# A hybrid diffusion backbone on one core: gate panels of the HGRN2 heads moved two heads back, the heads' read-out turned a head later

## The reference, cut to what matters

```python
q, zf, zb, v, g = split(h @ w_in)             # five parts of 1024 columns, 128 of each per head
log_f = log(lb + (1 - lb) * sigmoid(z)); k = (1 - lb) * sigmoid(-z)     # for zf and for zb
q = silu(q)
o = scan(q, kf, v, log_ff) + flip(scan(flip(q), flip(kb), flip(v), flip(log_fb)))
o = rmsnorm(o, gn_w)                          # over the 128 columns of each head
y = (o * silu(g)) @ w_out
```

## Time and profile before

| what | value |
|---|---|
| median of three runs | 2356.78 us (2351.39 to 2359.17) |
| the profiled execution, its own time | 2360.58 us |
| its span, first to last instruction | 2358.3 us |
| around the span | 2.3 us |
| mean granted TensorE clock | 0.948 |
| TensorE busy | 2155.7 us, 91% |
| VectorE, ScalarE busy | 1092.3 and 844.7 us |
| head panels and scans | from 75 to 609 us |
| output product | from 609.6 us on |

### The profile page before, as it was taken

How to read it: one execution, slowest core, us unless ns; L and a number is a source line. 1 busy time by engine, 2 the same in 40 slices (tenths; PEclk the granted TensorE clock), 3 DMA queues, 4 the chain that set the end, 5 groups by cost and what they waited for, 6 DMA issues and landing times.

```text
span 2358.3 us, 34131 instructions
## 1 busy us (share of the span) xinstructions
PE 2155.7 (91%) x13412; PEld 1918.5 (81%) x13412; DVE 1092.3 (46%) x1596; ACT 844.7 (36%) x1281; POOL 46.6 (2%) x72
## 2 busy tenths in 40 slices
PE   5999998997899999999999599999997598999998
PEld 3888888886789999999999597777774487888887
DVE  5654455556453222222234657667666435333334
ACT  2543334443224331122222344637373324542222
POOL 1000000000000000000000100000000000000000
PEclk8999999998899999999999799999998599999999
DMA  7322221221323332234321121211111232332332
GB/s 283 104 76 78 73 81 55 81 72 54 116 81 107 107 115 66 77 107 128 97 74 48 46 80 37 72 36 44 54 53 36 89 98 70 94 104 89 98 106 73
DMA packets 296564, 198.08 MB, mean 84 GB/s; under 512 B 4900, under 2 KB 288925, under 8 KB 295837
## 3 DMA queue, kind: packets, MB, share of 16 engines
q1 hardware_dynamic: 293965, 180.03, 24.9%
q0 software_dynamic: 2512, 16.80, 1.8%
HBM read 186.32 MB, written 10.49 MB: 83 GB/s over the span
## 4 chain that ended last, share of the span: by engine, by line
PE 76%; issue 8%; DVE 8%; ACT 5%; DMA 1%; POOL 1%; SPq 0%; ACTq 0%; DVEq 0%; POOLq 0%
PE G L281 65%; PE G L385 2%; PE S L1364 1%; PE S L729 1%; DVE hlo L614 1%; ACT e L1253 1%; PE S L703 1%; PE S L1360 1%; ACT whi L266 1%; DVE hn L606 1%; POOL rstd L588 1%; DVE cum L887 1%; PE G L391 1%; DMA xin<-in_ctx_dram 1%; PE S L577 1%
## 5 line engine op out<-in xcount | busy, mean ns | idle before, releaser
L281 PE MATMUL G<-hhi,whi 128*128 128x384 f32 (+2 forms) x2336 | 733.9, 372 | 36.1 <-DVE hlo L614 19.9
L270 DVE TENSOR_TENSOR wlo<-raw,whi 128x1024 fp32r<-128x1024 f32 (+1 forms) x225 | 288.1, 1281 | 869.2 <-ACT whi L266 869.0
L281 PE MATMUL G<-hlo,whi 128*128 128x384 f32 (+2 forms) x2336 | 685.8, 352 | 0.0
L281 PE MATMUL G<-hhi,wlo 128*128 128x384 f32 (+2 forms) x2336 | 685.2, 351 | 0.0
L266 ACT ACTIVATE whi<-raw 128x1024 fp32r<-128x1024 f32 (+1 forms) x225 | 248.8, 1106 | 978.1 <-PE G L281 505.6
L281 PEld LDWEIGHTS G<-hhi,whi 128*128 128x128 f32 x2336 | 427.6, 193 | 103.4 <-issue 45.0
L281 PEld LDWEIGHTS G<-hhi,wlo 128*128 128x128 f32 x2336 | 437.1, 192 | 20.4
L281 PEld LDWEIGHTS G<-hlo,whi 128*128 128x128 f32 x2336 | 437.8, 192 | 17.9
L281 PE MATMUL G<-mhi,whi 128*128 128x384 f32 (+2 forms) x694 | 219.6, 352 | 13.9 <-DVE mlo L1659 13.9
L281 PE MATMUL G<-mlo,whi 128*128 128x384 f32 (+2 forms) x694 | 218.6, 351 | 0.0
L281 PE MATMUL G<-mhi,wlo 128*128 128x384 f32 (+2 forms) x694 | 218.5, 351 | 0.0
(11 more groups left out here) (259 smaller groups left out, 1904.0 us busy)
## 6 DMA issues: line engine op xcount, KB each, us to landing
raw<-in_ffn_w_in_dram SPq DMA_DIRECT2D x88, 512.0 KB, 3.6
raw<-in_ffn_w_out_dram SPq DMA_DIRECT2D x32, 704.0 KB, 4.3
raw<-in_ssm_w_in_dram SPq DMA_DIRECT2D x41, 512.0 KB, 3.7
raw<-in_hg_w_in_dram SPq DMA_DIRECT2D x40, 512.0 KB, 3.8
adaw<-in_ada_w_dram SPq DMA_DIRECT2D x20, 1024.0 KB, 6.3
adaf<-in_ada_w_dram SPq DMA_DIRECT2D x20, 1024.0 KB, 5.1
ada<-in_ada_w_dram SPq DMA_DIRECT2D x4, 2048.0 KB, 13.3
raw<-in_ssm_w_out_dram SPq DMA_DIRECT2D x16, 512.0 KB, 3.2
```

Source lines behind the costliest of these rows:

```text
L270: dve.tensor_tensor(wlo[pn.slot][:, 0:kt, :], raw[pn.slot][:, 0:kt, :], f32(whi[pn.slot][:, 0:kt, :]), ALU.subtract).then_inc(s["lo"], 1)
L281: ins = pe.matmul(G[:, tl.slot, g0:g0 + n], w[pn.slot][:, k, :], r[:, k_base + k, t0:t0 + n], start=(first and k == 0 and i == 0), stop=(l ...
```

## The change

The gate becomes the first kind of panel in a call, and belongs to the head two before the other four: the calls for heads 0 and 1 have four panels, those for heads 2 to 7 five (gate of hn_ - 2 first), and the last call has two panels, the gates of heads 6 and 7, beside head 7's scan. The loop over heads now has two turns, and five calls are written out beside it (three before). Step 9 leaves the end of the fifth panel: head h's `osb` is turned at `TURN_AT`, after block 7 of the backward panel of the next call, and `gated` multiplies it there on VectorE, ahead of the `cum` scans. Step 2 waits for `osn`, as PAIR[1] is now read up to then. Slab loads stand in the same SP stream; the first of a head now waits for the head before to have finished its backward panel.

The output product's first two panels are interleaved block by block; the first six heads are split while TensorE does the last head's outputs, head 6 is turned in the last call, and head 7 is turned between blocks 5 and 6. The rest of the output product is as before.

```diff
+        GATE, QUERY, FWD, BWD, VALUE = range(5)
+        HG_OFF = [4 * D, 0, D, 2 * D, 3 * D]
+        FULL, NO_GATE, GATES = (GATE, QUERY, FWD, BWD, VALUE), (None, QUERY, FWD, BWD, VALUE), (GATE, GATE, None, None, None)
...
             if step == 1:
-                pe.wait_ge(s["og0"], h + 1)
-                v = hp + 4
+                pe.wait_ge(s["og0"], 1 if isinstance(h, int) and h == 0 else h)
...
                 if step == 3:
                     pe.wait_ge(s["vtm"], h + 1)
+                elif not isinstance(h, int) or h:
+                    pe.wait_ge(s["osn"], h)
...
+        def hg_tensor_turn(pe, h):
+            pe.wait_ge(s["osn"], h + 1)
+            for b in range(NBLK):
+                ins = pe.transpose(block(PAIR[0], b), block(m["osb"][:, :], b), ident[:, :])
+            ins.then_inc(s["turned"], 1)
...
-        STEP_AT = {(0, 5): 1, (1, 0): 2, (1, 3): 3, (1, 6): 4, (2, 1): 5, (2, 3): 6, (2, 5): 7, (4, 7): 9}
+        STEP_AT = {(0, 5): 1, (1, 0): 2, (1, 3): 3, (1, 6): 4, (2, 1): 5, (2, 3): 6, (2, 5): 7}
         OUT_AT = {(2, 7): 0, (3, 1): 1, (3, 3): 2, (3, 4): 3, (3, 5): 4, (3, 6): 5}
+        TURN_AT = (3, 7)
+        EARLY = HEADS - 2
...
+        def hgo_tensor_first(pe):
+            pn = At(PAN_HGO)
+            product_begin(pe, pn, pn)
+            product_begin(pe, pn + 1, pn + 1)
+            for k in range(KT):
+                if k == EARLY:
+                    hg_tensor_turn(pe, HEADS - 1)
+                pe.wait_ge(s["osp_lo"], k + 1)
+                first = product_block(pe, pn, pn, m["hhi"], m["hlo"], k, KT, SEGS)
+                if k == KT - 1:
+                    product_end(pe, pn, first, rows=SL_HGO)
+                ins = product_block(pe, pn + 1, pn + 1, m["hhi"], m["hlo"], k, KT, SEGS)
+            product_end(pe, pn + 1, ins, turn=m["mrow0"])
...
+                if j == 3 and hn_ is None:
+                    act.wait_ge(s["og0"], 1 + EARLY)
+                    act.wait_ge(s["pan"], PAN_HGO)
+                    for head in range(EARLY):
+                        og_hi(act, head)
...
+                if j == 4 and hn_ is None:
+                    for head in range(EARLY, HEADS):
+                        act.wait_ge(s["og0"], head + 2)
+                        og_hi(act, head)
...
+            def gated(head, gate):
+                dve.wait_ge(s["turned"], head + 1)
+                dve.wait_ge(took[gate.slot], gate.turn + 1)
+                dve.scalar_tensor_tensor(m["og"][:, bass.ds(head, 1), :].rearrange("p a t -> p (a t)"),
+                                         PAIR[0][:, 0:T], m["colA"][:, COL_GN:COL_GN + 1], gs[gate.slot][:, :],
+                                         ALU.mult, ALU.mult).then_inc(s["og0"], 1)
...
+                if j == 3 and hn_ is None:
+                    for head in range(EARLY):
+                        og_lo(dve, head)
...
+                    if hl is not None:
+                        gated(hl, pn)
                     for d in (0, 1):
                         back = slice(None, None, -1 if d else 1)
...
-                if j == 4 and h is not None:
-                    step_done(dve, h, 9)
-                    dve.scalar_tensor_tensor(m["og"][:, bass.ds(h, 1), :].rearrange("p a t -> p (a t)"),
-                                             PAIR[0][:, 0:T], m["colA"][:, COL_GN:COL_GN + 1], gs[ps_par][:, :],
-                                             ALU.mult, ALU.mult).then_inc(s["og0"], 1)
+                elif j == 4:
+                    og_lo(dve, hl)
+                    gated(h, pn + 1)
+                    og_lo(dve, h)
...
-            one(At(PAN_HG), 0, None, None, 0, 0)
-            with eng.Fori(0, (HEADS - 2) // 2) as i:
+            one(At(0), NO_GATE, 0, None, None, None, None)
+            one(At(4), NO_GATE, 1, At(3), 3, 0, None)
+            one(At(8), FULL, 2, At(7), 3, 1, 0)
+            with eng.Fori(0, (HEADS - 4) // 2) as i:
                 for u in (0, 1):
-                    one(At(PAN_HG + 5 * (u + 1), i * 5), i * 2 + (u + 1), At(PAN_HG + 5 * u, i * 5), i * 2 + u,
-                        1 - u, u)
-            one(At(PAN_HG + 5 * (HEADS - 1)), HEADS - 1, At(PAN_HG + 5 * (HEADS - 2)), HEADS - 2, 1, 0)
-            one(None, None, At(PAN_HG + 5 * (HEADS - 1)), HEADS - 1, 0, 1)
+                    one(At(13 + 5 * u, i * 5), FULL, i * 2 + (3 + u), At(12 + 5 * u, i * 5), 4,
+                        i * 2 + (2 + u), i * 2 + (1 + u))
+            one(At(33), FULL, 7, At(32), 4, 6, 5)
+            one(At(38), GATES, None, At(37), 4, 7, 6)
...
-                        if j == 1:
-                            slab_load(sp, 0, hn_ * (2 * SLAB) + 2 * D, None if h is None else hp + 2)
-                        if j == 4:
-                            slab_load(sp, 0, hn_ * (2 * SLAB) + (2 * D + SLAB), hg)
+                    if lot == 1 and hn_ is not None:
+                        slab_load(sp, 0, hn_ * (2 * SLAB) + 2 * D, None if h is None else pn + (-2))
+                if hn_ is not None:
+                    slab_load(sp, 0, hn_ * (2 * SLAB) + (2 * D + SLAB), pn)
```

More of the change, by code:

```diff
@@ L197, in program @@
             x sq sqd part gat ssum stat rstd rbc hn hhi hlo
-            sig lf cum dif ex kd qk vtm kdtm step cp att sf sb osq osr osn og0 osp_hi osp_lo
+            sig lf cum dif ex kd qk vtm kdtm step cp att sf sb osq osr osn turned og0 osp_hi osp_lo
             mhi mlo
@@ L739, in scan @@
             def scan(j, k):
                 if h is not None and (j, k) in STEP_AT:
-                    hg_tensor_scan(pe, hp, h, STEP_AT[j, k])
+                    hg_tensor_scan(pe, v, h, STEP_AT[j, k])
                 if h is not None and (j, k) in OUT_AT:
                     hg_tensor_out(pe, h, OUT_AT[j, k])
+                if hl is not None and (j, k) == TURN_AT:
+                    hg_tensor_turn(pe, hl)
             if h is None:
-                product_pair(pe, 0, hg, hg, SEGS, rows=hn_ * 2, turn=m["mrow0"])
@@ L747, in hg_tensor @@
[L747 to L753, removed]
+                product_pair(pe, 0, pn, pn, SEGS, rows=0, turn=m["mrow0"])
+            for j in range(3 if h is None else 0, 5):
+                if kinds[j] is None:
@@ L754, in hg_tensor @@
                     for k in range(KT):
                         scan(j, k)
-        def step_done(eng, h, step):
[L758 to L766, removed]
+                else:
+                    p = hg_panel(pn, kinds, j)
+                    lot = j - (kinds[0] is None)
+                    product(pe, p, p, m["hhi"], m["hlo"], KT, SEGS,
+                            rows=hn_ * 2 + lot // 2 if lot in (0, 2) and hn_ is not None else None,
+                            turn=m["mrow0"] if lot in (1, 3) and hn_ is not None else None,
+                            between=lambda k: scan(j, k))
@@ new lines, in og_hi, with og_lo, hg_scalar, take @@
+        def og_hi(act, j):
+            act.activation(m["hhi"][:, j, :], m["og"][:, j, :], ACT.Copy).then_inc(s["osp_hi"], 1)
+        def og_lo(dve, j):
+            dve.wait_ge(s["osp_hi"], j + 1)
+            dve.tensor_tensor(m["hlo"][:, j, :], m["og"][:, j, :], f32(m["hhi"][:, j, :]), ALU.subtract)\
+                .then_inc(s["osp_lo"], 1)
+        def step_done(eng, h, step):
+            eng.wait_ge(s["step"], 8 * h + step)
+        def hg_scalar(act, pn, kinds, hn_, v, vlot, h, hl):
+            def take(j):
+                p, kind, lot = hg_panel(pn, kinds, j), kinds[j], j - (kinds[0] is None)
+                split_hi(act, p + 2, KT)
+                tile = g_tokens(p.slot, T)
+                if kind == QUERY:
@@ L769, in take, with slab_turned @@
                     ins = act.activation(as_halves(m["qs"][:, :], T), tile, ACT.Silu)
[L770 to L773, removed]
-                else:
[L775 to L784, removed]
+                elif kind == GATE:
+                    ins = act.activation(as_halves(gs[p.slot][:, :], T), tile, ACT.Silu)
+                else:
+                    ins = act.activation(as_halves(th[kind - FWD][:, :], T), tile, ACT.Tanh, scale=0.5)
+                if hn_ is not None and lot in (0, 2):
+                    ins = act.activation(in_row(m["mrow0"]), slab_rows_of(p.slot), ACT.Copy)
+                elif hn_ is not None and lot in (1, 3):
+                    ins = slab_turned(hn_, lot, p)
+                ins.then_inc(took[p.slot], 1)
+            def slab_turned(head, lot, p):
+                for b in (0, 1):
+                    t = head * 4 + ((lot - 1) + b)
+                    ins = act.activation(m["mods"][:, 0, bass.ds(t + 2 * KT, 1), :].rearrange("p a c -> p (a c)"),
+                                         spare(p.slot, 0)[:, 2 * b:2 * b + 2], ACT.Identity,
+                                         bias=m["colB"][:, bass.ds(t + 2 * KT, 1)])
+                return ins
             def decays(head, d):
@@ L796, in hg_scalar @@
             for j in range(5):
-                if j and hg is not None:
-                    take(hg + (j - 1), j - 1)
```

(15 more changed lines are left out.)

49 lines of the change are left out of this document (20 added, 29 removed).

## The result

The changed kernel took **2320.74 us** in the median of four runs (2316.78 to 2326.0), the kernel before 2357.98 (2351.39 to 2361.07, four runs). The ratio is 0.985, with a 95% interval of 0.9824 to 0.9875: 37 us less, 1.5%. The profiled execution of the changed kernel took 2326.0 us, the slowest of its four.

What follows compares the result with a forecast made beforehand. TensorE was taken to bound the kernel, standing idle at head ends and in the last head's tail. Net 36 between heads, minus 7 at the first boundary, plus 7 in the tail: 36 us less, 2321 us, range 2308 to 2338.

Steps and rivals of the forecast that it cites:

- Between the heads: Layer 0's mixer, six boundaries: removing TensorE's stall at the `osb` turn saves 44 us, 8 left for waits and loop turn; net 36.
- 44 - 8 - 7: Heads: 44 us from removed stalls, less 8 for `vT` waits and the loop's turn, less 7 at the first boundary.
- The fit of `gated` into VectorE's pause: Between `th` and the `cum` scans: `gated`, 1.02 us, fits VectorE's 1.06 us idle; otherwise the `vT` wait would be 1.7.
- the loop's one turn: Turn back of the loop over heads: charged 3.3 us of idle and 1.2 of slow clock, 4.5 together, covering its `vT`.
- The waits for `vT`: Before step 1 of each head TensorE waits 0.7 us for the value take-out; five boundaries make 3.7 us.
- The first boundary: Head 0's step 1, no panel ahead: TensorE waits 5.4 us for `vT`, then restarts slowly, 1.6 more; minus 7 us.
- The tail: Last value panel to output panel 2: 74.8 us less 16.9 saved ahead, 57.9 against 65.2; net 7 us gained.
- The slab's load beside that of `x1`: Next pair's slab load, released amid the `x1` load: 1.5 us taken, bounds nothing and 3.4; interleaving on shared engines nearer 3.
- chains between the heads a little long: Rival, chance 0.16: 3 us instead of 0.7 at each of six boundaries and the slab's full price; gain 20, 2337 us.
- restart cheaper: Rival, chance 0.16: outputs at full clock take about 5 us instead of 10.7, and 2 more elsewhere; gain 44, 2313 us.
- clock taking it back: Rival, chance 0.04: granted clock falls elsewhere as TensorE's idle goes, mean down 0.014 from 0.948; no change, 2356 us.
- the ring on ScalarE: Rival, chance 0.04: ScalarE's in-order queue makes `vT` bound every head; slower, 2372 us at 8 us of wait per boundary.

Runs made afterwards that it cites:

- putting the wait back: Changed kernel with TensorE again waiting, at the end of each head's last panel, until `osb` is written: 2357.83 us, 0.9984 of the kernel before.
- the last two experiments: Loop over heads written out without jumps: on the changed kernel with TensorE's `osb` wait put back, 2350.06 us (one run); on the changed kernel alone, 2319.72 us.
- Moving the steps: Changed kernel with head 0's scan steps later in head 1's call, step 1 after block 4 of the query panel: 2311.82 us, 0.9802 of the kernel before.
- the late splits: Changed kernel with the splits of heads 0 to 5 moved behind the last head's square and mean: 2318.68 us, 0.9835 of the kernel before.
- four other traces: Changed kernel with head 0's steps later (2311.82 us), `osb` wait put back with the loop (2357.83) and without (2350.06), first six heads' splits late (2318.68).

## Why the prediction was right, point by point

**Between the heads: right.** I put a full head at 59.0 + 0.7 and it took 60.1. From before to after, the root of head 6 moved from 564.9 to 518.6; with two panels less ahead of it (16.9) that is 29.4, and my 44 - 8 - 7 was 29. By parts: the first boundary lost 7.4 (158.3 for 167.7 at head 0's root, two panels less ahead), the six boundaries behind it gained 36.8 for my 36. That the stall was worth more than its idle time is what putting the wait back shows. The fit of `gated` into VectorE's pause held: in the chain of the changed kernel `og` takes 0.93 us and `cum` follows at once. (The last line is output panel 2, 48 matmuls, 8.43 when undisturbed.)

```profile
513.23 0.93 DVE og L902
514.16 3.31 DVE cum L955 x2
...
588.22 10.42 PE G L288 x48
```

One item inside it was wrong: I charged 4.5 us for the loop's one turn. It cost 0.9 of idle. Those 3.3 us stood bare because TensorE had waited just before, as the last two experiments show on the changed kernel; I had taken them for a cost of the jump itself. "ISA Cache" in Advanced Engine Details and Errata of the Trainium skill gives only the size of TensorE's cache and its two lines; that a long loop is fetched anew at each turn was my inference from it. The runs don't contradict it, 4.1 us went with the jump, but it leaves out what can hide that time, and this decided here. The waits for `vT` came to 4.5 in sum, for five that I put at 3.7 (five times 0.7 is 3.5), and took back part of what I had overcharged. That the net was so close owes something to these two errors.

**The first boundary: right.** 5.2 us of wait, foreseen 5.4, and the slow restart: 7.4 in all for my 7. Moving the steps gave back about 7.

**The tail: the mechanism right, some sizes off.** From the end of the gate panels, 538.6, I had the first output at + 8.4, the output product at + 20.3, the turn of head 7 at + 34.5, the load at + 46.9 and the turn of panel 1 at + 50.3. It was 8.3, 20.1, 32.5, 45.2 and 48.6. The main difference is one restart: the product began at full clock (1.00 in the window from 558.5), where the kernel before restarted slowly at its start; the clock had risen during the turn of head 6. The slow restart after the wait of 8.8 was real, 10.42 for a panel instead of 8.43, 2.0 where I had 1.6. Output panel 2 started at 588.2, where I had said near 593.

The slab's load beside that of `x1` was put at 1.5 and cost the latter 0.2: 10.4 for 10.2 before. It was the slab that gave way: 9.0 us for 5.1, and nothing waited for it. By "Issuing engines are not separate DMA queues" in DMA: Bandwidth & Descriptors of the Trainium skill the two interleave, and the trace agrees, since both were under way from 577.4 on and the slab took 3.9 longer; the estimate of 3 us for the load of `x1` made from it does not hold.

**The sum.** 36 us foreseen, 39.2 at the landmark (29.4 between the heads and 9.9 in the tail, for 29 and 7), 37.2 between the medians. That the median fell within 1 us of my 2321 is luck: behind the landmark alone 5.2 us were lost in the profiled execution. The rivals, one by one: chains between the heads a little long (no, 60.1), restart cheaper (in the changed kernel at the start of the output product only, some 2 us; amid the outputs in four other traces, 3 us), clock taking it back (no, the mean granted clock rose from 0.948 to 0.951), and the ring on ScalarE (no).

## What to carry to other kernels

A stall of the busiest engine costs its idle time, a restart at half clock, and whatever the engine's queue had been hiding, such as a loop's jump. Here a stall of 4.4 us made a head 5 us longer, although it also covered 0.9 of another wait, and at the jump 10 us longer. So a wait that is short but periodic is worth moving by a whole stage, even when that needs the order of the panels changed. And when a product is split over two accumulators to cover a late operand, ask what is released by the late operand: here a load that needed the very cover that the interleaving used up. Either the plain order or the load started earlier was 8 us better.

## What the runs showed that I had not expected

Layer 1's code is the same in all of these kernels, yet its mixer, taken from GpSimd's last root of the norm ahead of it to the first root of the norm behind it, lasts from 660.7 to 673.8 us in the twelve profiled executions. Two of them, the changed kernel's and that of the late splits (length, busy times of PE, PEld, DVE, ACT and POOL, granted clock, DMA):

```profile
1257.00:1930.50 673.50, 577.68 (x2694) 468.22 (x2709) 407.95 (x568) 306.04 (x592) 16.75 (x33) 0.89 0.20 59
```

```profile
1256.60:1917.30 660.70, 566.53 (x2708) 459.40 (x2709) 408.57 (x568) 305.75 (x592) 16.68 (x33) 0.90 0.20 60
```

VectorE and ScalarE have the same busy time; TensorE has 11 us more in the longer one, at a clock of 0.89 against 0.90. The likely cause is where the clock rises and falls among layer 1's many short stretches; that was not tested. For differences under 10 us a landmark in the trace was a better measure than the whole time.
